# Unscaled tokens for the first two feature tiles of each perceptron, and another order around its norm

## The reference

```python
def mlp(s, shift, scale_m):
    hm = rms_norm(s, g_norm2) * (1.0 + scale_m) + shift
    return jnp.square(jax.nn.relu(hm @ w_mlp1)) @ w_mlp2

x_new = x + gt1 * (y @ w_out)                 # "out": the residual step before the norm
x_new = x_new + gt2 * mlp(x_new, sh2, sc2)    # 1024 -> 4096 -> 1024
```

## Time and profile before

| | us |
|---|---|
| median of 3 runs | 2635.66 |
| lowest, highest | 2634.33, 2643.11 |
| profiled execution, its own time | 2639.13 |
| its span | 2637.3 |
| TensorE busy | 2484.3 (94%) |
| VectorE busy | 1559.2 (59%) |
| ScalarE busy | 933.8 (35%) |

### The profile page before, as it was taken

One profiled execution on the slowest core, in us unless ns is written; L12 is line 12 of the kernel. 1 busy time (PEld: TensorE's weight loads), 2 busy tenths in 40 slices (PEclk: granted clock), 3 DMA queues, 4 the chain that ended last, 5 costly groups with the idle time before them and its releaser, 6 DMA issues.

```text
span 2637.3 us, 45579 instructions
## 1 busy us (share of the span) xinstructions
PE 2484.3 (94%) x19508; PEld 2019.8 (77%) x19508; DVE 1559.2 (59%) x2412; ACT 933.8 (35%) x1596; POOL 115.0 (4%) x220
## 2 busy tenths in 40 slices
PE   6999887779999999999998999999999998999997
PEld 4777666667887888877777888888887776788886
DVE  4555567767656888854674566544445466544444
ACT  4544433323235323342553422222223354422322
POOL 0000001111100000000000000000000000000000
PEclk8999899989999999999999999999999999999999
DMA  6100000004643555311002123333321102222210
GB/s 281 64 1 1 33 4 4 4 32 174 233 180 132 184 197 202 148 44 64 1 33 95 49 104 125 131 128 128 128 89 44 64 33 93 87 101 104 96 64 33
DMA packets 32345, 244.87 MB, mean 93 GB/s; under 512 B 3632, under 2 KB 3792, under 8 KB 21008
## 3 DMA queue, kind: packets, MB, share of 16 engines
q1 hardware_dynamic: 12240, 167.97, 15.9%
q0 software_dynamic: 19904, 73.97, 8.9%
HBM read 239.83 MB, written 2.10 MB: 92 GB/s over the span
## 4 chain that ended last, share of the span: by engine, by line
PE 86%; DVE 8%; issue 2%; ACT 2%; DMA 1%; POOL 0%; SPq 0%; DVEq 0%; ACTq 0%
PE ps L346 57%; PE ps L2294 3%; PE ps L2523 2%; PE ps L1474 1%; PE ps L2551 1%; PE ps L1052 1%; PE ps L2567 1%; PE ps L376 1%; PE ps L2569 1%; PE ps L2568 1%; PE ps L377 1%; PE ps L1008 1%; PE ps L378 1%; PE ps L1054 1%; PE ps L1053 1%
## 5 line engine op out<-in xcount | busy, mean ns | idle before, releaser
L346 PE MATMUL ps<-hh,ws 128*128 128x512 f32 x3168 | 735.8, 391 | 3.8 <-DVE xT L1911 3.2
L346 PEld LDWEIGHTS ps<-hh,ws 128*128 128x128 f32 x3168 | 591.1, 188 | 130.7 <-issue 8.2
L327 ACT ACTIVATE ws<-raw 128x1024 fp32r<-128x1024 f32 x295 | 309.2, 1051 | 419.8 <-PE ps L346 386.3
L335 DVE TENSOR_TENSOR ws<-raw,ws 128x1024 fp32r<-128x1024 f32 x295 | 359.8, 1221 | 155.4 <-ACT ws L327 155.4
L346 PE MATMUL ps<-g,ws 128*128 128x512 f32 x1536 | 355.1, 390 | 0.0
L346 PEld LDWEIGHTS ps<-g,ws 128*128 128x128 f32 x1536 | 286.1, 188 | 58.1
L346 PE MATMUL ps<-gg,ws 128*128 128x512 f32 x960 | 221.5, 391 | 2.1 <-ACT ws L327 2.1
L1911 DVE SCALAR_TENSOR_TENSOR xT<-ps,mods,xT 128x512 f32<-128x512 f32 x120 | 90.0, 750 | 211.9 <-PE ps L346 204.6
L346 PEld LDWEIGHTS ps<-gg,ws 128*128 128x128 f32 x960 | 181.2, 189 | 40.6 <-ACT ws L327 2.5
L2074 DVE TENSOR_TENSOR sq<-sq 128x512 f32<-128x512 f32 (+1 forms) x128 | 80.0, 625 | 138.2 <-ACT sq L2051 138.2
L2051 ACT ACTIVATE sq<-ps 128x512 f32<-128x512 f32 (+1 forms) x128 | 69.5, 543 | 250.0 <-PE ps L346 234.0
(11 more groups left out here) (393 smaller groups left out, 3616.8 us busy)
## 6 DMA issues: line engine op xcount, KB each, us to landing
raw<-in_w_m SPq DMA_DIRECT2D x32, 2048.0 KB, 7.9
raw<-in_w_ada POOLq DMA_DIRECT2D x80, 512.0 KB, 3.9
raw<-in_w_mlp SPq DMA_DIRECT2D x16, 2048.0 KB, 7.9
ar<-in_w_ada POOLq DMA_DIRECT2D x48, 512.0 KB, 3.9
raw<-in_w_in SPq DMA_DIRECT2D x8, 2048.0 KB, 7.4
raw<-in_w_mg SPq DMA_DIRECT2D x8, 1536.0 KB, 7.3
raw<-in_w_out SPq DMA_DIRECT2D x6, 2048.0 KB, 8.1
raw<-in_w SPq DMA_DIRECT2D x5, 2048.0 KB, 8.5
```

The costliest lines, as they stand in the source:

```text
L327: e.activation(w_of(n)[0], pieces[n][2], ACT.Copy).then_inc(*hi(n))
L335: e.tensor_tensor(l, pieces[n][2], h.bitcast(F32), ALU.subtract).then_inc(*lo(n))
L346: m = e.matmul(o, a, b, start=n == 0, stop=n == 3 * kt - 1)
```

## The change

- **Unscaled tokens.** While out runs, ScalarE and VectorE also write `z` = x times gain, unnormed, as high and low part, into the buffer that later holds the hidden features (`act_z`, `dve_z`). u tiles 0 and 1 of x multiply z in place of the normed h. What is missing is made good afterwards: VectorE multiplies the product by the root (`"scaled"`), and ScalarE's relu adds as bias the product of the weights with the shift. That product is made in out by `dve_shift` (one product of 1024 columns and three additions of 512, 256 and 128 columns, once for each of the two weight pieces) and `pe_shift` (two matmuls of 4 columns).
- **Statistics inside the tiles.** `pe_stat` for x stands inside `pe_tiles`, after the first two features. In in2 of layer 2 likewise, and there q0 comes after u3 and k0.
- **Splits inside the norm.** Piece 2 is split ahead of the root, piece 3 between the norm's sixth and seventh feature tile, piece 4 in iteration 1 of the loop.
- **Layer 2's out.** The context's tiles 6 and 7 stand in front of x's tiles 6 and 7, and the context's norm between them. u tile 2 takes the context first.

```diff
-        def pe_tiles(e, ns, names, rhs, w, order, ready):
-            lhs = [pe_piece(e, n) for n in ns]
+        def pe_tiles(e, ns, names, rhs, w, order, ready, middle=None):
+            lhs = {}
             for name in names:
                 for t in ps.take(name):
                     e.wait_ge(*t)
             for i, k in order:
+                if i not in lhs:
+                    lhs[i] = pe_piece(e, ns[i])
+                if middle is not None and (i, k) == (0, 2):
+                    middle()
...
+        def act_first_norm(e, n, tag, bv, dst, bufs):
+            act_norm(e, tag, bv, dst, bufs, range(6))
+            split_hi(e, n)
+            act_norm(e, tag, bv, dst, bufs, range(6, KT))
+        def dve_first_norm(e, n, *args):
+            steps = dve_norm_steps(e, *args)
+            for _ in range(9):
+                next(steps)
+            split_lo(e, n)
+            for _ in steps:
+                pass
...
+        def act_z(e, tag, z, gain, m):
+            e.activation(z[:, 0, m, :], xT[:, m, :], ACT.Identity, scale=gain(m)).then_inc(*act((tag, "zhi", m)))
+        def dve_z(e, tag, z, gain, m):
+            e.wait_ge(*act[tag, "zhi", m])
+            e.scalar_tensor_tensor(z[:, 1, m, :], xT[:, m, :], gain(m), z[:, 0, m, :].bitcast(F32), ALU.mult,
+                                   ALU.subtract).then_inc(*dve(((tag, "z"), m)))
+        def dve_shift(e, tag, i, md, buf):
+            name, slot, w, _, _ = pieces[first[f"{tag}u0"] + i]
+            e.wait_ge(*raw_in[slot][name])
+            e.tensor_tensor(buf.rearrange("p (k c) -> p k c", k=KT), w, md[:, 24:32, 0:1].to_broadcast([P, KT, 128]),
+                            ALU.mult).then_inc(*dve())
+            for n in (512, 256, 128):
+                e.wait_ge(*dve.prev())
+                e.tensor_tensor(buf[:, 0:n], buf[:, 0:n], buf[:, n:2 * n], ALU.add).then_inc(*dve((tag, "part", i)))
+        def pe_shift(e, tag, bufs):
+            for t in ps.take((tag, "shift"), (7,)):
+                e.wait_ge(*t)
+            ps.n -= 1
+            for i in range(2):
+                e.wait_ge(*dve[tag, "part", i])
+                m = e.matmul(ps[tag, "shift"][:, 4 * i:4 * i + 4], bufs[i][:, 0:128], ones[:, 0:4], start=True, stop=True)
...
         def tensor_out1(e):
             ps.use = range(7)
             for m in range(8):
+                if m == 7:
+                    pe_shift(e, "m0", shift_1)
                 pe_tile(e, first["out0"] + m, [(("out", m), of(yy), T, "yy" if m == 0 else None)])
-            pe_stat(e, "x2", T, SQX, (7,))
...
-            def tensor(e, ready):
+            def tensor(e, ready, stat):
                 beside = aside[3](e) if aside and len(aside) > 3 else iter(())
+                ps.use = range(8 - len(rows_))
                 for j, h, hid, x, w, bufs, bank in by_size:
                     n = start("u", 0)
-                    pe_tiles(e, [n, n + 1], [(tag, "u", 0, m, j) for m in range(2)], of(h), w, by_feature, ready[j])
+                    pe_tiles(e, [n, n + 1], [(tag, "u", 0, m, j) for m in range(2)], of(h if j else hid), w, by_feature,
+                             ready[j] if j else (tag, "z"), middle=None if j else lambda: stat(e))
+                ps.use = range(8)
...
-                        pe_tile(e, start("u", q) + m, [((tag, "u", q, m, j), of(h), w, None)
-                                                       for j, h, hid, x, w, bufs, bank in rows_])
+                        early = q == 0 and m == 2
+                        pe_tile(e, start("u", q) + m, [((tag, "u", q, m, j), of(h), w, ready[j] if early else None)
+                                                       for j, h, hid, x, w, bufs, bank in (by_size if early else rows_)])
...
-                        split_hi(e, start("u", q) + m + 2)
+                        split_hi(e, start("u", q) + m + 2 + (q == 0 and m == 1))
                         for j, h, hid, x, w, bufs, bank in rows_:
...
+                            if j == 0 and 8 * q + m < 2:
+                                e.wait_ge(*dve[tag, "scaled", m])
+                                e.activation(r, r, ACT.Relu, bias=SHIFT[:, m:m + 1]).then_inc(*act((tag, "u", q, m, j)))
...
+                            if j == 0 and 8 * q + m < 2:
+                                e.wait_ge(*acc[tag, "u", 0, 1, 0])
+                                e.wait_ge(*dve.prev())
+                                e.tensor_tensor(r, ps[tag, "u", 0, m, 0][:, 0:w], rs[:, 0:w], ALU.mult).then_inc(
+                                    *dve((tag, "scaled", m)))
...
-                for m in range(2, 8):
-                    end = m == 7 and not last
-                    pe_tile(e, n + m, [((l, "out", m, j), of(h), w, None)
-                                       for j, h, hid, x, w, bufs, bank in out_rows[::-1 if end else 1]],
-                            middle=(lambda: pe_row_stat(e, (l, "so"), out_rows[1])) if end else None)
-                pe_row_stat(e, (l, "so"), out_rows[0])
+                for m in range(2, 8 if last else 6):
+                    if m == 7:
+                        pe_shift(e, mtag, shift_2)
+                    pe_tile(e, n + m, [((l, "out", m, j), of(h), w, None) for j, h, hid, x, w, bufs, bank in out_rows])
+                if not last:
+                    pe_shift(e, mtag, shift_2)
+                    for m in (6, 7):
+                        pe_tile(e, n + m, [((l, "out", m, 1), of(hc2), TC, None)])
+                    for m in (6, 7):
+                        pe_tile(e, n + m, [((l, "out", m, 0), of(hh), T, None)],
+                                middle=None if m == 7 else lambda: pe_row_stat(e, (l, "so"), out_rows[1]))
...
+                    dve_keep_shift(e, mtag)
+                    dve_out(6, out_rows[1])
+                    dve_out(7, out_rows[1])
+                    steps = dve_norm_steps(e, (l, "mx", 1), ctx2, rsc2, gains[1], shift2(md, 1), hc2, bufs_m[1], (l, "so", 1))
+                    for _ in range(7):
+                        next(steps)
+                    dve_out(6, out_rows[0])
+                    split_lo(e, n + 9)
+                    dve_out(7, out_rows[0])
```

More of the change, by code:

```diff
@@ L1933, in scalar_out1 @@
                 act_square(e, "x2", m, xT[:, m, :], SQX)
+                act_z(e, "m0", gg, gain2, m)
         def vector_out1(e):
@@ L2067, in vector @@
                     for m in range(8):
-                        split_lo(e, start("u", q) + m + 2)
+                        split_lo(e, start("u", q) + m + 2 + (q == 0 and m == 1))
                         for row in rows_:
@@ L2271, in tensor_in2 @@
                       if name == "k" or not last]
-                pe_tiles(e, [n + i for i, _ in cn], [name for _, name in cn], of(hc2), TC,
-                         [(i, k) for k in range(KT) for i in range(len(cn))], tc)
+                if last:
+                    pe_tiles(e, [n + 1], [(l, "k", 0, 1)], of(hc2), TC, [(0, k) for k in range(KT)], tc)
+                else:
+                    ps.n += 1
+                    pe_tiles(e, [n, n + 1, n + 2], [name for _, name in cn], of(hc2), TC,
+                             by_feature + [(2, k) for k in range(KT)], tc,
+                             middle=lambda: pe_stat(e, xs, T, SQX, (7,)))
+                    ps.n -= 1
                 pe_tiles(e, [n, n + 1], [(l, "u", 3, 0), (l, "k", 0, 0)], of(hh), T, by_feature, tx)
@@ L2824, in scalar_out2, with act_out @@
                 meet(e, act, (l, "attention"))
-                for m in range(8):
-                    split_hi(e, first[f"o{l}0"] + m + 2)
-                    for j, h, hid, x, w, bufs, bank in out_rows[::-1 if m == 7 else 1]:
-                        e.wait_ge(*dve[l, "out", m, j])
-                        act_square(e, (l, "so", j), m, x[:, m, 0:w], bufs)
+                n = first[f"o{l}0"]
+                def act_out(m, row):
+                    j, h, hid, x, w, bufs, bank = row
+                    e.wait_ge(*dve[l, "out", m, j])
+                    act_square(e, (l, "so", j), m, x[:, m, 0:w], bufs)
+                    if j == 0:
+                        act_z(e, mtag, g2, gain2, m)
+                for m in range(8 if last else 6):
+                    split_hi(e, n + m + 2)
+                    for row in out_rows:
+                        act_out(m, row)
+                if not last:
+                    split_hi(e, n + 8)
+                    act_out(6, out_rows[1])
+                    act_out(7, out_rows[1])
+                    act_rms(e, (l, "so", 1), TC, rsc2)
+                    act_norm(e, (l, "mx", 1), shift2(md, 1), hc2, bufs_m[1], range(6))
+                    act_out(6, out_rows[0])
+                    split_hi(e, n + 9)
+                    act_out(7, out_rows[0])
+                    act_norm(e, (l, "mx", 1), shift2(md, 1), hc2, bufs_m[1], range(6, KT))
             def vector_out2(e):
@@ L2833, in vector_out2, with dve_out @@
                 meet(e, dve, (l, "attention"))
-                for m in range(8):
```

(27 more changed lines are left out.)

56 lines of the change are left out of this document (36 added, 20 removed).

## The result

| | before | after |
|---|---|---|
| median (4 runs each, side by side) | 2635.86 us | 2655.30 us |
| profiled execution, its own time | 2639.13 | 2653.89 |
| its span | 2637.3 | 2652.1 |

The account below looks back on a forecast made before the run. TensorE, 86% of the chain, was taken as the bound. M0 -1.0, in2 +2.7, m1 -20.5 and m2 +5.3 make 13.5 us slower: median 2649.2 us from 2635.66, profiled execution 2652.6, range 2640 to 2655.

Parts of the forecast that it names:

- m0, up to u tile 2: From out1's end into m0: u tile 2 starts at 802.5 instead of 810.3; 7 us won so far.
- m0, behind that: M0 at tile 5: TensorE waits 5.1 us for its split, plus 2.3 us slow clock; m0 loses 1.0 us overall.
- Later iterations keep up: M0 after tile 5: the ScalarE and VectorE loop delays TensorE no further; no cost counted.
- in2: In2 of layer 2: nothing is waited for, 10.3 us instead of 13.0; 2.7 us won.
- m1, the shift: Layer 2's out, behind tile 5: TensorE waits 4.1 us at pe_shift for dve_shift, plus 2.3 us slow clock.
- m1, the bank: M1, u tile 2: TensorE waits 15.1 us for bank 0, until x's u tile 1 relu at 1507.8; 2.3 us slow clock.
- m2: M2: u tile 2 ends 6.3 us earlier, piece 5 comes 1.0 late; 5.3 us won.
- Low clock behind the three pauses and nowhere else: Sign in the changed profile: low clock behind waits of 4.1, 5.1 and 15.1 us, nowhere else that it was not before.
- the clock did fall after all three pauses: Rival, m0 and m1: clock stays up or falls for less, three times 2.3 us not paid, 2642.3; chance 0.12.
- the bank wait was not short: Rival, m1: relu of u tile 1 comes in time, 3.3 us wait for piece 5 instead; no change, 2635; chance 0.05.
- the loop in m0 did not catch up: Rival, m0: the ScalarE and VectorE loop catches up, 7 us more are kept, 2641; chance 0.03.
- All four gaps close: Rival, m0, in2, m1 and m2: gains of 7.1, 2.7, about 4 and 6.3; 20 us faster, 2615.6; chance 0.04.

Follow-up runs that it names:

- e3: After, with ScalarE and VectorE splitting each piece one iteration earlier in every perceptron's first way up; ratio to before 1.0060.
- e7: Before, with only the change's part in in2 of layer 2 put in; 1827.11 us from m0's start to the last matmul, before 1833.18.
- e2: After, with layer 2's shift product moved behind the context's tiles 6 and 7, its VectorE read behind their residuals; ratio to before 1.0035.
- e1: After, with m1's u tiles 2 and 3 given the four free PSUM banks, later tiles the rest in order of release; ratio to before 1.0021.
- e9: After, with free banks in m1, later shift product, earlier splits, modulation begun eight tiles later and m1's products dealt out anew; median 2616.77 us, ratio to before 0.9942.
- e10: As e9, but without the earlier splits: pieces behind piece 4 are split where after splits them; ratio to before 0.9947.
- e4: The kernel before, unedited, profiled once more; 2631.47 us in one execution.

## Why the prediction was right, point by point

It forecast 13.5 us more; the two profiled executions differ by 14.8 us and the medians by 19.4. From m0's start on, two pairs of executions give 14.8 and 15.0, so the loss is of that size. The other 4.6 us between the medians are how these executions fell: before's profiled one lay 3.3 us above its median and after's 1.4 below. The traces put such scatter ahead of m0, but the executions that were not profiled have none. It leaves after's median, 2655.30, 6.1 us above the forecast of 2649.2 and 0.3 past the upper end of the range (2655), and the profiled execution, 2653.89, 1.3 above its 2652.6.

- **m0, up to u tile 2**: 802.5 forecast, 802.05 measured, where before it was 810.30. The shift's product cost 0.36 us (0.3) without a wait (0.1).
- **m0, behind that**: tile 4 forecast for 814.8, measured 814.39; tile 5 forecast for 825.4 after 5.1 us, measured 825.10 after 5.00. The slow clock cost 1.9 us, not 2.3. M0 neither won nor lost (0.1 won; 1.0 lost forecast). "Later iterations keep up" was right only because TensorE was late. E3 shows that there was about 1 us to spare at hidden tile 7.
- **in2**: 10.12 us (10.3), 2.9 us won (2.7), and e7 wins the same alone.
- **m1, the shift**: 4.02 us (4.1) with 2.1 of clock (2.3); e2 took both away and won 6.5. The split of piece 1: 0.76 us (0.8).
- **m1, the bank**: 15.19 us (15.1), 2.3 us of clock (2.3). TensorE starts again at 1506.92, and 1507.8 was forecast, but the two can't be set side by side as they stand. The forecast counted on from before's times, where out tile 5 ends at 1451.65; in after it ends at 1447.99, 3.66 us earlier. Set on the same footing the measured time is 1510.6. The forecast also left the slow clock behind the first pause out of this chain and added it at the end; with it in, 1510.1. E1 shows by another choice of banks that no other wait is near: the next comes three tiles later. The step that found it reads the rotation of banks, not the profile, in which such a wait can't be seen before it exists.
- **m2**: tile 2 to tile 5 waits 0.38 and 1.14 us (1.0 forecast for the second). From m2's start to the last matmul, 355.0 us against 360.3: 5.3 won, as forecast.
- **What the sum lacked**: in2 of layer 3. Its first x matmul comes 0.36 us later after the first context matmul (7.95 instead of 7.59 us), since VectorE now stands 0.46 us ahead of x's norm (why, I did not trace), and the clock behind the wait was 0.72 instead of 1.00, which costs 1.7 us (19 matmuls in 6.0 us instead of 26). "Low clock behind the three pauses and nowhere else" was the sentence that failed. That the total is off by only 1.3 us is in part luck: the 2.1 us missing here and the 1.1 us too many charged to m0 work against each other.

The rivals: the clock did fall after all three pauses, for no longer than the forecast said; the bank wait was not short, and the loop in m0 did not catch up. In e1, where it was made short by force, m1 waited 3.87 us for piece 5, where the rival said 3.3 as m0 does; the rival's price was no change, and e1 is 5.1 us slower than before by the table, 2.6 of them the slow clock behind this wait. "All four gaps close" is nearly e9: 17.0 us less than before by the table, 15.3 by the ratio, where the rival said 20. It did need the bank free and the loops in step, and in step they came only when the modulation was moved. One reading in the prediction says more than its rows do: 13 and 9 slow matmuls are two places in one execution, so they can't bear on what differs from run to run.

## What to carry to other kernels

Work that is allowed to start before its norm holds its result, and so its bank, for the whole norm and what the reader does first. The reader here was a relu that no longer touched the bank (0.8 us), but most of the wait was the norm and the loop ahead of it. Count the banks that stay taken through that time, and let the next tiles take those that are free. Where a wait is cured and the time does not move, look at the end of the loop that fed it. Earlier splits won nothing in m0 while ScalarE and VectorE ended their loop at the same moment; taking four unrelated operations of 1.9 us out of that loop won 6.3 us in m0 alone (e10). With the bank, the shift, the splits and that loop repaired, a change that lost 0.6% wins 0.6%.

## What the runs showed of the hardware

- In the four windows behind waits the granted clock repeated when the program was run again: 0.59, 0.59, 0.60 and 0.72 in after, 0.59, 0.59, 0.58 and 0.72 in its second execution. It does not follow from the length of the wait: behind 4.3 us it cost 2.7 us in before's m0 and 1.4 in e7's, behind 1.90 us it was 0.72 in after, and behind 1.79 us in e3 it was 1.00:

```profile
2036.83:2042.83 6.00, 6.00 (x27) 1.00 0.00 0
```

  What sets it is open. The Trainium skill, "TensorE: Matmul & The Clock Gate", section "What's actually happening", says that the point at which the clock rises differs from run to run. Between kernels the rows agree. Two executions of one program differ ahead of m0, as the page says (0.88 in before and 0.93 in e4 from 300 to 400 us), but in the four windows above by no more than 0.02. One stretch behind m0 did differ: behind the first context matmuls in layer 3's in2 the kernel before had 0.50 and e4 0.72, hidden by the wait for x's norm.
- The part of the program ahead of m0 took from 780.0 to 792.9 us in the thirteen profiles. Where two kernels differ by less than 10 us, a stage's rows tell more than a few times of the whole.
